# A hybrid decoder trunk on one core: another order within a slot on three engines, and the probabilities divided on ScalarE

## What is computed

```
z = rmsnorm(x) @ w_in                          # 3328 columns: q, k, v, gate a, conv B, C, h, conv gate
q, k = rope(q), rope(k)                        # 8 query heads, 2 key heads, 64 wide
s = q @ k.T * SCALE, banded: a block of 128 queries sees its own and the previous 128 keys
p = exp(s - m) / (sum(exp(s - m)) + exp(sink - m))
o = p @ v
u = C * h;  y = B * causal_conv3(u)            # the other branch
mix = concat(o * silu(ga), y * silu(gc))
x = x + mix @ w_out
x = x + sigmoid(x @ w_pg) * (p_i @ w_pp)
```

## Time and profile before

| | |
|---|---|
| median of 3 runs | 1227.17 us (1225.5 to 1230.06) |
| profiled execution | 1228.82 us, span 1227.1 us |
| TensorE busy | 1155.2 us, 94% of the span |
| VectorE busy | 718.1 us, 59% |
| ScalarE busy | 455.9 us, 37% |
| GpSimd busy | 485.3 us, 40% |
| mean granted TensorE clock | 0.984 of full speed |

### The profile page before, as it was taken

How to read it: one execution, slowest core, us unless ns; L and a number is a source line. 1 busy time by engine, 2 the same in 40 slices (tenths; PEclk the granted TensorE clock), 3 DMA queues, 4 the chain that set the end, 5 groups by cost and what they waited for, 6 DMA issues and landing times.

```text
span 1227.1 us, 18672 instructions
## 1 busy us (share of the span) xinstructions
PE 1155.2 (94%) x7302; PEld 1134.0 (92%) x7302; DVE 718.1 (59%) x1290; ACT 455.9 (37%) x973; POOL 485.3 (40%) x627
## 2 busy tenths in 40 slices
PE   5998998898889999999999999899797999999996
PEld 5998997888889999999999999789797999999996
DVE  3454687787764444466643477878676454444554
ACT  5312355444453222333321125444544332223333
POOL 3554253646553322233434333555364433222220
PEclk9999999998999999999999999999899999999999
DMA  8622110111111212111163211111011122121103
GB/s 217 171 71 53 35 53 18 35 36 35 35 36 29 80 53 62 43 44 44 35 173 98 60 35 36 35 35 36 18 36 35 41 70 64 47 65 44 44 1 142
DMA packets 127951, 70.44 MB, mean 57 GB/s; under 512 B 43156, under 2 KB 123860, under 8 KB 127832
## 3 DMA queue, kind: packets, MB, share of 16 engines
q1 hardware_dynamic: 122400, 61.33, 17.6%
q10 hardware_dynamic: 5464, 7.92, 2.6%
HBM read 59.10 MB, written 6.76 MB: 54 GB/s over the span
## 4 chain that ended last, share of the span: by engine, by line
PE 75%; DVE 12%; ACT 5%; POOL 4%; issue 2%; DMA 1%; ACTq 1%; DVEq 0%
PE ring L421 68%; PE aux L458 2%; DVE yc L1161 2%; PE aux L435 1%; POOL ws L404 1%; DVE kst L1067 1%; DMA xnat<-in_x_prompt_dram 1%; POOL pw L376 1%; POOL pw L379 1%; DVE qst L1064 1%; DVE up L1157 1%; PE aux L444 1%; DVE yc L1159 1%; DVE st L1036 1%; DVE pw L1075 1%
## 5 line engine op out<-in xcount | busy, mean ns | idle before, releaser
L421 PE MATMUL ring<-act,ws 128*128 128x352 f32 x6048 | 1000.6, 323 | 0.7 <-DVE kT L1108 0.3
L421 PEld LDWEIGHTS ring<-act,ws 128*128 128x128 f32 x6048 | 970.3, 189 | 3.5 <-DVE act L952 0.6
L404 POOL TENSOR_TENSOR ws<-stage,ws 128x256 fp32r<-128x256 f32 x352 | 284.9, 841 | 579.1 <-ACT ws L685 579.1
L694 ACT ACTIVATE act<-tmp 128x352 fp32r<-128x352 f32 x120 | 59.7, 498 | 247.7 <-DVE tmp L1195 143.6
L398 POOL TENSOR_TENSOR stage<-stage,gT 128x256 f32<-128x256 f32 x208 | 135.9, 683 | 22.6 <-DMA stage<-in_w_in_dram 12.2
L685 ACT ACTIVATE ws<-stage 128x1024 fp32r<-128x1024 f32 (+1 forms) x84 | 91.5, 1090 | 85.1 <-PE ring L421 78.4
L945 DVE TENSOR_TENSOR act<-tmp,act 128x352 fp32r<-128x352 f32 x120 | 72.3, 602 | 52.8 <-ACT act L694 52.0
L376 POOL TENSOR_SCALAR_AFFINE_SELECT pw<-pw 128x1024 fp32r<-128x1024 f32 x28 | 34.0, 1213 | 97.6 <-DVE pw L1075 97.6
L1215 DVE TENSOR_TENSOR tmp<-ring,gate 128x352 f32<-128x352 f32 x48 | 25.2, 525 | 79.2 <-ACT gate L877 77.8
L777 ACT ACTIVATE gate<-gate 128x352 f32<-128x352 f32 x48 | 23.8, 497 | 121.9 <-DVE gate L1115 96.3
L1193 DVE TENSOR_TENSOR tmp<-ring,act 128x352 f32<-128x352 f32 x48 | 25.2, 525 | 66.8 <-PE ring L421 66.8
(11 more groups left out here) (184 smaller groups left out, 1065.5 us busy)
## 6 DMA issues: line engine op xcount, KB each, us to landing
stage<-in_w_in_dram SPq DMA_DIRECT2D x36, 512.0 KB, 3.9
stage<-in_w_in_dram SPq DMA_DIRECT2D x32, 256.0 KB, 3.8
stage<-in_w_pg_dram SPq DMA_DIRECT2D x16, 512.0 KB, 3.7
rot<-raw ACTq DMA_DIRECT2D x32, 132.0 KB, 2.4
stage<-in_w_out_dram SPq DMA_DIRECT2D x32, 128.0 KB, 2.9
stage<-in_w_out_dram SPq DMA_DIRECT2D x16, 256.0 KB, 3.1
out_dram<-xnat SPq DMA_DIRECT2D x8, 512.0 KB, 4.3
xnat<-in_x_prompt_dram SPq DMA_DIRECT2D x4, 512.0 KB, 8.0
```

What stands on the lines that cost most here:

```text
L404: rest = nc.gpsimd.tensor_tensor(ws[:, s, 1, k:k + 2, :], stage[:, s, k:k + 2, :], ws[:, s, 0, k:k + 2, :].bitcast(F32), ALU.subtract)
L421: mm = nc.tensor.matmul(out, ws[:, w % 2, wp, kw, :], x[:, xp, kx, cs], start=(i == 0 and wp == 0 and xp == 0), stop=(i == n - 1 and wp == 1))
L694: nc.scalar.activation(dst, tmp[:, s % 2, :], ACT.Copy).then_inc(S["hi_out"], 1)
```

## The change

Five things change. On ScalarE `exps` and `split` move from behind the slot's copies to the slot's start, ahead of `Silu`, and a new `norm` block stands ahead of `Silu` as well: four copies of 128x128, each scaled by one column of reciprocals. On VectorE `divide` keeps the sum and the reciprocal and loses the 128x512 multiplication; `probs_low` moves from behind `divide` and `take_o` to the slot's start, and `scores_of` from ahead of the convolution and gate work to the slot's end. On GpSimd the masks of a slot that begins a tile move: before they stood behind the low part of the previous weight tile and ahead of the next scaling, now they stand ahead of that low part, behind the scaling that precedes it. Units start every 12/5 slots from slot 26 instead of every 5/2 from slot 25. The transposes of v and the sample units come one slot later.

```diff
-    BCAST, KC_TURN, SC_TURN, QPACK, V_TURN = (3, 2), 7, 8, 17, 18
-    D0, AT0 = 19, 25
+    BCAST, KC_TURN, SC_TURN, QPACK, V_TURN = (3, 2), 7, 8, 17, 19
+    D0, AT0 = 20, 26
...
-        return AT0 + 5 * u // 2
+        return AT0 + 12 * u // 5
...
-                    masks(l, f, (0,))
                     pool.wait_ge(loaded[s], loaded_count(w))
...
-                    masks(l, f, (1, 2))
+                    masks(l, f, (1, 2, 3))
...
-                            for g in range(g0 + s - NCH, g0 + s):
+                            for g in range(g0 + 15, g0 + 18):
...
+                    for u in at_slot(s, exps=1):
+                        sc.wait_ge(S["negm_done"], 2 * (count(l, u) + 1))
+                        cb = combs[u % 2]
+                        for t in range(4):
+                            nc.scalar.activation(cb[:, t, :], cb[:, t, :], ACT.Exp, bias=st[:, 1, t:t + 1],
+                                                 scale=SCALE, accum_out=st[:, 4, t:t + 1]).then_inc(S["exp_done"], 1)
+                        nc.scalar.activation(st[:, 3, :], st[:, 2, :], ACT.Exp).then_inc(S["exp_done"], 1)
+                    for u in at_slot(s, split=-3):
...
+                    for u in at_slot(s, norm=2):
+                        sc.wait_ge(S["inverse_ready"], l * 2 * NB + u + 1)
+                        for t in range(4):
+                            scaled = nc.scalar.activation(combs[u % 2][:, t, :], combs[u % 2][:, t, :], ACT.Copy,
+                                                          scale=st[:, 6, t:t + 1])
+                        scaled.then_inc(S["probs_ready"], 1)
                     if kind in ("gc", "ga"):
...
-                    for u in at_slot(s, split=-3):
...
-                    for u in at_slot(s, exps=1):
...
                 def divide(l, u):
 
-                    cb = combs[u % 2]
                     ve.wait_ge(S["exp_done"], exps(l, u))
                     link(V.tensor_tensor(st[:, 5, :], st[:, 4, :], st[:, 3, :], ALU.add))
-                    link(V.reciprocal(st[:, 6, :], st[:, 5, :]))
-                    V.tensor_tensor(cb, cb, st[:, 6, :].rearrange("p (a n) -> p a n", n=1).to_broadcast([P, 4, P]),
-                                    ALU.mult).then_inc(S["probs_ready"], 1)
+                    ve.wait_ge(S["probs_ready"], count(l, u))
+                    V.reciprocal(st[:, 6, :], st[:, 5, :]).then_inc(S["inverse_ready"], 1)
...
+                    for u in at_slot(s, low=5):
+                        probs_low(l, u)
                     for gg in decode_at(s, 2):
                         decode_divide(l, gg)
...
-                    for u in at_slot(s, low=5):
-                        probs_low(l, u)
...
-                    for u in at_slot(s, scores=0):
-                        scores_of(l, u)
...
+                    for u in at_slot(s, scores=0):
+                        scores_of(l, u)
```

More of the change, by code:

```diff
@@ L237, in hybrid_trunk @@
             rot_in roped tables_in v_turned v_hi v_taken v_lo kc_in kc_turned kc_taken sc_in sc_turned sc_taken
-            vc_in q_packed cur_taken qk_hi qk_lo scores_done scores_taken negm_done exp_done probs_ready
+            vc_in q_packed cur_taken qk_hi qk_lo scores_done scores_taken negm_done exp_done probs_ready inverse_ready
             p_turned pt_taken ph_done pl_done masked pv_done o_shifted o_taken dcache_done dcache_taken
@@ L735, in _ @@
                         split_weights(w + 1)
+                    for u in at_slot(s, exps=1):
[6 more added lines that the diff above has]
+                    for u in at_slot(s, split=-3):
+                        b, gg = u // 2, u % 2
+                        own, other = slice(gg * HD, (gg + 1) * HD), slice((1 - gg) * HD, (2 - gg) * HD)
+                        if u < 2:
+                            sc.wait_ge(S["roped"], 5 * (l + 1))
+                        else:
+                            sc.wait_ge(S["scores_done"], count(l, u - 2) + 1)
+                        tok = slice(b * P, (b + 1) * P)
+                        key = slice(b % 2 * P, (b % 2 + 1) * P)
+                        nc.scalar.activation(qst[own, gg, :, :], raw[m][own, :, tok], ACT.Copy).then_inc(S["qk_hi"], 1)
+                        nc.scalar.activation(kst[own, gg, 0, key], kT[own, tok], ACT.Copy).then_inc(S["qk_hi"], 1)
+                        nc.scalar.activation(kst[other, gg, 0, key], kT[own, tok], ACT.Copy).then_inc(S["qk_hi"], 1)
                     if s and A_TILES[(s - 1) // NCH][0] == "ga":
@@ L815, in _ @@
                         nc.scalar.activation(st[:, 3, 0:1], st[:, 2, 0:1], ACT.Exp).then_inc(S["exp_done"], 1)
-                    for u in at_slot(s, exps=1):
-                        sc.wait_ge(S["negm_done"], 2 * (count(l, u) + 1))
-                        cb = combs[u % 2]
-                        for t in range(4):
-                            nc.scalar.activation(cb[:, t, :], cb[:, t, :], ACT.Exp, bias=st[:, 1, t:t + 1],
-                                                 scale=SCALE, accum_out=st[:, 4, t:t + 1]).then_inc(S["exp_done"], 1)
-                        nc.scalar.activation(st[:, 3, :], st[:, 2, :], ACT.Exp).then_inc(S["exp_done"], 1)
                     for gg in decode_at(s, 0):
```

## The result

The changed kernel takes 1182.63 us (median of 4 runs, 1181.35 to 1184.18) against 1228.62 us before (4 runs): a ratio of 0.9625, 95% interval 0.9591 to 0.9658. The profiled execution has a span of 1179.6 us, 47.5 less than before.

A forecast was written before the change was run, and what follows sets the result against it. TensorE, busy 94% of the span, was taken as the bound. From 1227.1 us, 61.6 of waits, clock and restarts gone gave 1165.5; 12.5 remaining gave 1178.0, range 1168 to 1192 (0.60), 8 in 10 within 1165 to 1202.

The forecast's parts named there:

- The bound: TensorE, busy for 94% of the span; only its idle time, 45.3 us of it mask waits, and its clock could be gained.
- the cycle: ScalarE and VectorE queue heads waiting on each other (exponentials behind Silu), not work, were said to make the 45.3 us stalls.
- The floor: Time if all mask waits, their clock and restarts and the v transposes' wait went: 1227.1 - 61.6 = 1165.5 us.
- the 3.3 us of v: TensorE's one wait at the v transposes (L582), expected to go when they come one slot later: 3.3 us.
- What stays: Mask waits left at `pv`: 1.0 us at units 3, 8, 13, 0.5 at 5 and 10, 0.1 elsewhere; 9.8 in sum.
- The walk: Timing the changed order by hand through slots 45 to 56; masks 0.7 to 1.9 us late at slot 51, VectorE never pausing.
- The scaled copies: Four copies on ScalarE replace VectorE's multiplication: 0.3 us each, 1.2 a unit, hidden unless others queue behind them.
- The places of the units: Units every 12/5 slots match the tile pattern, so each unit meets the same kind of slot every round; no separate gain priced.
- The scores behind the convolution: On VectorE, evictions and convolution go first; maxima up to 2.1 us later, which "costs nothing by itself".
- the one in which VectorE stays late: Rival: late scores and closer units make the walk some 2 us slower, 36 us of waits, about 1202 us; chance 0.17.
- The slower rival: ScalarE's wait for the reciprocal, ahead of Silu and high copy, closes a new cycle: 0.5% slower or about 1250; chance 0.05.
- the drain: About 1.38 us more per ScalarE table load, delaying exponentials of units 5 and 10: 1184 us; chance 0.02.

The follow-up runs named there:

- b1: Kernel before with only the exponentials moved to the start of ScalarE's slot, ahead of Silu and split: 1202.53 us, 0.9797 of the kernel before.
- e1: Changed kernel with the exponentials put back behind Silu and the slot's copies: 1197.22 us, 0.9755 of the kernel before.
- e6: Changed kernel with the old places of the units (every 5/2 slots from slot 25, v transposes at slot 18): 1203.89 us, 0.9812 of the kernel before.
- e2: Changed kernel with the multiplication by the reciprocals back on VectorE and no scaled copies on ScalarE: 1197.59 us, 0.9757 of the kernel before.
- n1: Changed kernel with four extra 28-column scaled copies on ScalarE ahead of the four that count: 1186.16 us, 0.9672 of the kernel before.
- e3: Changed kernel with scores_of put back ahead of the convolution and gate work: 1179.94 us, 0.9611 of the kernel before.
- e4: Changed kernel with the low part put back behind divide and take_o on VectorE: 1184.49 us, 0.9650 of the kernel before.
- e5: Changed kernel with GpSimd's masks of a tile's first slot put back behind the low weights: 1185.38 us, 0.9659 of the kernel before.

## Why the prediction was right, point by point

**The bound and the cycle: the bound right, the cycle half of it.** The waits fell to under 15 us, none over 3, and b1 and e1 move them by moving the exponentials alone: 25 us on the old kernel, 16 on the new one. But "not work" was wrong: at unit 8 the cycle was 2.24 of the 7.37 us, the 2.29 that VectorE waited, and in b1 the other 5.13 stand where VectorE works without a pause but for the split. The other edits had to shorten that queue, and none of them had a price of its own in my sum. The forecast of 49 us less against 46 measured is right in size because all stalls but small ones went, for whatever reason; the shares were not foreseen. In the sum I had the waits down by 35.5 us and 13.6 for the rest; the spans give 33.6 and 13.9.

**The floor and the 3.3 us of v.** The waits went down by 33.6 us, the span by 47.5; 13.9 are clock, restarts and the v transposes. The 3.3 us of v in them were not the change's: in b1 and e6 the transposes stand at slot 18 as before, and no wait for them appears. In the profiled execution of before VectorE had waited 4.5 us for one rotated transfer:

```profile
98.33 1.79 DVE L1126 TENSOR_TENSOR rot<-rot,sinT 128x1056 f32<-128x1056 f32 x1 [4.54 <-DMA rot<-raw]
```

So it belongs to that execution and not to the slot, and one occurrence in two layers should have warned me. The term had the wrong cause; that the profiled execution of before held these 3.3 us is luck for the sum.

**What stays: right in place, short in size.** I walked to units 3, 8 and 13 and took 1.0 us each, with up to 1.9; measured are 1.42 to 2.32. Units 5 and 10, 0.5 each in the sum, do not stall. In all 9.8 foreseen, 11.7 measured. The walk lost the time at "it never pauses there": VectorE waits 1.40 us for the copy of `pv` (195.43), behind late exponentials, a table load and the first Silu. On the walk's clock, zero at 167.74 (the turn at 23.6 is 191.34), the low part was due to start at 29.7, 197.44, and starts at 199.04, 1.6 us later. That no stall would touch the clock was wrong too: three of six do, so the clock is not at 1.00 through both stretches.

**The median.** It lies 4.6 us above 1178.0. Of these, 1.6 are the span's. Another 1.75 are the step from span to time: 1181.35 - 1179.6 here, 1228.82 - 1227.1 before. I had set span and median equal because they agreed by chance, the median of the three runs being lower than the run that was profiled. The last 1.3 are the spread of the four runs.

**The scaled copies: right in price, wrong as to what they are for.** 1.29 us a unit, where I took 1.2. But I counted them as a cost that is hidden and gave the relief of VectorE no price; e2 shows it as 16 us, as large as the exponentials' place, since one of the two multiplications before the low part takes 1.40 us there instead of 0.69 and shifts all that follows. n1 shows that ScalarE has little room: at unit 3 only 0.2 of 0.94 us more stay hidden.

**The places of the units.** I noted that they meet the same slots in every round and used it for the walk alone. They are worth 23 us in the changed kernel and nothing in the old one. Exponentials and places together on the old kernel were not run.

**The scores behind the convolution**: "costs nothing by itself" is doubtful: the late maxima are behind the 1.40 us pause, and e3 has 3.7 us less span, though its median is not shown to be lower. **The low part first**: right in kind, 4.1 us of span in e4, not clear of the noise. **The masks on GpSimd**: close to nothing, as e5 shows.

**Rivals.** Of the one in which VectorE stays late a part came, 0.4 to 1.3 us a stall more than I took. The slower rival's wait of ScalarE for the reciprocal is 9.2 us in all (5.5 and 3.7 in eight waits), too small to close a new cycle. Of the drain that the Trainium skill adds to every table load (ScalarE: Activation LUTs, What ACT_TABLE_LOAD costs) nothing shows after the change either: the load of L801 stands at 192.98 in the timeline, 1.28 us long, and the Silu starts at 194.28.

## What to carry to other kernels

In programs that run in written order, look for an instruction that is ready but stands behind one that waits for the other engine; if the other engine in turn waits for it, moving it can be worth much (25 us here). Then count how much of the stall the cycle explains: the wait inside it (2.29 us) was less than a third of the stall (7.37), and the rest was the length of a queue. Gains of such edits don't add: exponentials and places gave 25 and 0 us alone on the old kernel, and 16 and 23 when taken from the new one, so undo and do each alone. And look whether a stall that you price at its length also costs clock: about half of what e1 and e2 lost by their spans was not in the waits.

## What the hardware showed that I had not expected

Some of VectorE's instructions stretch beside GpSimd: the same 128x512 multiplication, with both operands in SBUF, took 1.40 us beside the masks and 0.69 without, the two 64x128 subtractions 2.23 and 0.60 together. The low part, which reads one operand from the `aux` bank, took 0.67 to 0.69 us in either case. The granted clock does not follow the stall's length alone: 0.79 over 8 us behind a stall of 1.76, and 1.00 behind one of 2.77 and behind one of 1.97 at 770, where the window below was read. In n1 it was 1.00 behind four stalls of 2.70 to 2.79.

```profile
770.00:778.00 8.00, 7.99 (x51) 1.00 0.23 67
```

What else decides it stayed open.
